# Gate and up of a SwiGLU block as 2 by 2 block products with seven products, on one Trainium2 core

## The reference

```python
h = h + y @ w_out                                   # y: RWKV-7 and attention heads, 2048 wide
hn = rmsnorm(h, ffn_norm_g)
h = h + (silu(hn @ w_gate) * (hn @ w_up)) @ w_down  # 2048 -> 5632 -> 2048
e = rmsnorm(p @ ple_proj, ple_norm_g)               # p: 256 wide
gate = sigmoid(rmsnorm(h, ple_gate_norm_g) @ ple_gate_w + ple_gate_b)
h = h + gate * e
```

## Time and profile before

| | us |
|---|---|
| median of 3 runs | 2743.32 |
| lowest, highest run | 2742.16, 2745.13 |
| span of the profiled execution | 2740.7 |
| busy: PE, PEld, DVE, ACT, POOL | 2685.5, 2142.2, 1167.3, 1022.2, 220.5 |

### The profile page before, as it was taken

The page is one execution under the profiler, slowest core; times in us unless marked ns, Lnnn a source line. Parts: engine busy times, 40 slices in busy tenths (PEclk is TensorE's granted clock), DMA queues, the critical chain, the costliest instruction groups (busy, mean ns, idle before and its releaser), DMA issues.

```text
span 2740.7 us, 41126 instructions
## 1 busy us (share of the span) xinstructions
PE 2685.5 (98%) x15562; PEld 2142.2 (78%) x15562; DVE 1167.3 (43%) x1717; ACT 1022.2 (37%) x1460; POOL 220.5 (8%) x348
## 2 busy tenths in 40 slices
PE   7999999999999999999999999999999999999998
PEld 6776776776776788888888888888888888888787
DVE  6654653653653535333333333333333333334543
ACT  5445535534544425433223332233332222234421
POOL 3101200210111103000000000000000000011300
PEclk9999999999999999999999999999999999999999
DMA  5221231231132323322233222332223322233332
GB/s 169 87 77 63 68 90 59 70 86 63 63 95 95 125 92 108 105 92 99 81 95 108 98 99 82 96 105 99 95 85 95 108 99 92 94 87 108 105 120 75
DMA packets 108136, 255.91 MB, mean 93 GB/s; under 512 B 35288, under 2 KB 37848, under 8 KB 108024
## 3 DMA queue, kind: packets, MB, share of 16 engines
q1 hardware_dynamic: 105920, 247.10, 28.2%
q0 software_dynamic: 2112, 7.34, 0.8%
HBM read 245.43 MB, written 8.98 MB: 93 GB/s over the span
## 4 chain that ended last, share of the span: by engine, by line
PE 71%; issue 18%; POOL 3%; DVE 3%; ACT 2%; DMA 1%; SPq 1%; POOLq 0%; DVEq 0%; ACTq 0%
PE bank L318 23%; PE bank L315 23%; PE bank L319 23%; PE bank L356 1%; POOL probs L1097 1%; POOL scratch_pool L129 1%; DVE w_lo L310 1%; DMA raw<-w_mix 1%; ACT w_hi L303 1%; POOL sg_t L1089 0%; PE bank L481 0%; POOL carried L1124 0%; POOL M_t L1111 0%; PE bank L510 0%; SPq L1319 0%
## 5 line engine op out<-in xcount | busy, mean ns | idle before, releaser
L310 DVE TENSOR_TENSOR w_lo<-raw,w_hi 128x1024 fp32r<-128x1024 f32 (+1 forms) x484 | 546.0, 1130 | 966.2 <-ACT w_hi L303 965.5
L303 ACT ACTIVATE w_hi<-raw 128x1024 fp32r<-128x1024 f32 (+1 forms) x484 | 471.6, 975 | 964.6 <-PE bank L319 941.3
L315 PE MATMUL bank<-hn_hi,w_hi 128*128 128x512 f32 x1664 | 648.1, 389 | 0.0
L319 PE MATMUL bank<-hn_hi,w_lo 128*128 128x512 f32 x1664 | 647.3, 389 | 0.0
L318 PE MATMUL bank<-hn_lo,w_hi 128*128 128x512 f32 x1664 | 647.3, 389 | 0.0
L315 PE MATMUL bank<-in_hi,w_hi 128*128 128x512 f32 x1088 | 455.6, 419 | 30.3 <-DVE in_lo L1689 12.1
L318 PE MATMUL bank<-in_lo,w_hi 128*128 128x512 f32 x1088 | 440.8, 405 | 0.0
L319 PE MATMUL bank<-in_hi,w_lo 128*128 128x512 f32 x1088 | 427.7, 393 | 0.0
L318 PEld LDWEIGHTS bank<-hn_lo,w_hi 128*128 128x128 f32 x1664 | 312.4, 188 | 65.4 <-issue 0.5
L315 PEld LDWEIGHTS bank<-hn_hi,w_hi 128*128 128x128 f32 x1664 | 312.4, 188 | 65.0 <-issue 0.5
L319 PEld LDWEIGHTS bank<-hn_hi,w_lo 128*128 128x128 f32 x1664 | 312.4, 188 | 64.8
(11 more groups left out here) (240 smaller groups left out, 2120.6 us busy)
## 6 DMA issues: line engine op xcount, KB each, us to landing
raw<-w_gu SPq DMA_DIRECT2D x176, 512.0 KB, 3.4
raw<-w_mix SPq DMA_DIRECT2D x116, 512.0 KB, 3.6
raw<-w_down SPq DMA_DIRECT2D x64, 384.0 KB, 3.1
raw<-w_down SPq DMA_DIRECT2D x64, 320.0 KB, 2.8
raw<-ple_gate SPq DMA_DIRECT2D x32, 512.0 KB, 3.5
raw<-w_mix SPq DMA_DIRECT2D x28, 384.0 KB, 3.3
h_t<-xT SPq DMA_DIRECT2D x4, 1024.0 KB, 6.3
out<-h_t POOLq DMA_DIRECT2D x16, 256.0 KB, 2.3
```

What stands on the lines that cost most here:

```text
L303: nc.scalar.activation(w_hi[:, ring_slots(par2, half), 0:cols[half]], raw[:, half, 0:cols[half]], ACT.Copy).then_inc(hi_ready, 1)
L310: nc.vector.tensor_tensor(w_lo[:, s, 0:cols[half]], raw[:, half, 0:cols[half]], w_hi[:, s, 0:cols[half]].bitcast(F32), ALU.subtract).then_ ...
L315: nc.tensor.matmul(out, w_h, x_hi, start=start, stop=False, skip_group_check=True)
L319: return nc.tensor.matmul(out, w_l, x_hi, start=False, stop=stop, skip_group_check=True)
```

## The change

Gate and up, which were two products with the same input, become one product of 2 by 2 blocks. The row blocks of the weights are a gate tile and the up tile of the same 128 features; the column blocks are the even and the odd kt; the input is cut into even and odd kt and into the left and the right 256 tokens. The product of such blocks is formed with seven block products in place of eight (Winograd's form of Strassen's scheme). A block product is 8 kt with three matmuls of 256 columns each, 168 matmuls for a pair of tiles and 7,392 for the 44 pairs.

- The weights: seven blocks of 128 by 1024 per pair are rounded and subtracted. Three are loaded blocks, four are sums that POOL forms (`pool_sums`, 128x1024 each). The four loaded blocks of a pair (`raw_11`, `raw_12`, `raw_21`, `raw_22`) and the four sums lie where `h_t` lay.
- The input: for every two kt ACT writes the scaled values to `hf`, POOL forms four differences of 128x256 (`pool_x_sums`), ACT rounds blocks and differences, and DVE subtracts. `hf` and the differences `t123` have one buffer. The seven inputs lie in `x_a` and `x_c`.
- The results: DVE and ACT combine the banks (`dve_pair`, `act_copy_product`), then come norm factor, SiLU, product and split as before.
- The residual is stored to DRAM (`h_scratch`) and loaded again for the down projection; the activations of all 44 pairs are stored (`act_scratch`) and loaded by chunk, 5.77 MB each. `ple_proj` now stands between gate/up and down, its result is stored and loaded again (`e_scratch`). The down projection is four chunks in a row, and the gate of the embedding follows it directly.

The diff, cut to what the prediction speaks of:

```diff
-CHUNK_SLABS = 2 * CF + OUT_SLABS
-N_PROJ = N_FFN + CHUNKS * CHUNK_SLABS
+PAIRS = D_FF // P
+QUAD = 4
+KP = KT // 2
+TH = SEQ // 2
+PRODUCTS = 7
+RING = 4
+BLOCKS = PRODUCTS * PAIRS
+N_PROJ = N_FFN + BLOCKS // 2
...
+    raw_21 = sb_at(first + 66 * KB, "raw_21", [P, HALF * P])
+    raw_22 = [sb_at(first + (70 + 4 * i) * KB, f"raw_22_{i}", [P, HALF * P]) for i in range(2)]
+    raw_11 = [raw[:, 0, :], sb_at(first + 78 * KB, "raw_11_odd", [P, HALF * P])[:]]
+    raw_12 = raw[:, 1, :]
+    sums = [sb_at(first + (82 + 4 * i) * KB, f"sum_{i}", [P, HALF * P]) for i in range(4)]
...
+    def act_x_scaled(act, o):
+        i = o // 2
+        act.wait_ge(*added_late(o))
+        if i > 0:
+            act.wait_ge(S("x_summed_pool"), KT // 2 + 4 * i)
+            act.wait_ge(S("hn_ready"), 3 * i - 1)
...
+    def act_x_blocks(act, i):
+        act.wait_ge(S("hn_hi_ready"), 2 * i + 2)
+        nc.scalar.activation(x_hi[0][:, i, :], hf[:, 0, 0:TH], ACT.Copy).then_inc(S("in_hi_ready"), 1)
+        nc.scalar.activation(x_c[:, 0:2, i, :], by_half(hf[:, 1, :]), ACT.Copy).then_inc(S("in_hi_ready"), 1)
+
+    def act_x_sums(act, i):
+        act.wait_ge(S("x_summed_pool"), KT // 2 + 4 * i + 4)
+        nc.scalar.activation(x_a[:, 0:3, i, :], t123[:], ACT.Copy).then_inc(S("in_hi_ready"), 1)
...
+    def pool_x_sums(pool, i):
+        b11, b12, b21, b22 = hf[:, 0, 0:TH], hf[:, 0, TH:SEQ], hf[:, 1, 0:TH], hf[:, 1, TH:SEQ]
+        pool.wait_ge(S("hn_hi_ready"), 2 * i + 2)
+        if i > 0:
+            pool.wait_ge(S("hn_ready"), 3 * i)
+        nc.gpsimd.tensor_tensor(t123[:, 0, :], b12, b11, ALU.subtract).then_inc(S("x_summed_pool"), 1)
+        nc.gpsimd.tensor_tensor(t123[:, 2, :], b22, b12, ALU.subtract).then_inc(S("x_summed_pool"), 1)
+        pool.wait_ge(S("x_summed_pool"), KT // 2 + 4 * i + 1)
+        nc.gpsimd.tensor_tensor(t123[:, 1, :], b22, t123[:, 0, :], ALU.subtract).then_inc(S("x_summed_pool"), 1)
+        pool.wait_ge(S("x_summed_pool"), KT // 2 + 4 * i + 3)
+        nc.gpsimd.tensor_tensor(t4[:, i, :], b21, t123[:, 1, :], ALU.subtract).then_inc(S("x_summed_pool"), 1)
...
+    def pe_pair(pe, p, q, first=False):
+        banks = gu_banks(q)
+        for j in range(PRODUCTS):
+            pe.wait_ge(lo_ready, blocks(PRODUCTS * p + j + 1))
+            if j == 0 and not (isinstance(p, int) and p < 2):
+                pe.wait_ge(copied, 3 * p - 3)
+                pe.wait_ge(combined, 7 * p - 7)
+            if j == 3:
+                pe.wait_ge(copied, 3 * p + 1)
+            if j == 5:
+                pe.wait_ge(copied, 3 * p + 2)
+            if j == 6:
+                pe.wait_ge(combined, 7 * p + 3)
+            if first and j == 6:
+                pe.wait_ge(S("hn_ready"), 3 * KP + 1)
+            if first and j == 2:
+                pe.wait_ge(S("h_summed"), KT + 1)
+                nc.tensor.matmul(aux[:], ones[:], acc_h[:], start=True, stop=True, skip_group_check=True
+                                 ).then_inc(S("norm_summed"), 1)
+            out, slot = banks[bank_of[j]][:, 0:TH], gu_slot(q, j)
+            high, low = x_hi[x_of[j]], x_lo[x_of[j]]
+            for i in range(KP):
+                if first and j < 3:
+                    pe.wait_ge(S("hn_ready"), 3 * i + j + 1)
+                w_h, w_l = w_hi[:, slot, i * P:(i + 1) * P], w_lo[:, slot, i * P:(i + 1) * P]
+                nc.tensor.matmul(out, w_h, high[:, i, :], start=opens[j] and i == 0, stop=False, skip_group_check=True)
+                nc.tensor.matmul(out, w_h, low[:, i, :], start=False, stop=False, skip_group_check=True)
+                last = nc.tensor.matmul(out, w_l, high[:, i, :], start=False, stop=i == KP - 1, skip_group_check=True)
+            last.then_inc(weights_used, 1)
...
+    def act_pair(act, p, q, first=False, last=False):
+        for j in range(PRODUCTS):
+            if j in (0, 2, 3):
+                act_copy_product(act, p, q, j)
+            if first and j == 2:
+                rstd_of(act, rstd_h, NORM_FFN)
+            if j == 6:
+                act.wait_ge(combined, 7 * p + 5)
+                if not (isinstance(p, int) and p == 0):
+                    act.wait_ge(S("act_product_ready"), p)
+                nc.scalar.activation(silu_u[:], cg[:], ACT.Silu).then_inc(S("silu_ready"), 1)
+            if not (last and j + RING >= PRODUCTS):
+                act_round_block(act, *ahead(p, q, j))
+            if j == 0 and not (isinstance(p, int) and p == 0):
+                act_high_out(act, p - 1)
...
+    def dve_pair(dve, p, q, first=False, last=False):
+        a, b, c, d = (bank[:, 0:TH] for bank in gu_banks(q))
+        left, right = slice(0, TH), slice(TH, SEQ)
+        had_one = not (isinstance(p, int) and p == 0)
+        for j in range(PRODUCTS):
+            if j == 0 and had_one:
+                dve_product(dve, p - 1)
+            if j == 1:
+                dve.wait_ge(weights_used, blocks(PRODUCTS * p + 2))
+                dve.wait_ge(copied, 3 * p + 1)
+                if had_one:
+                    dve.wait_ge(S("silu_ready"), p)
+                nc.vector.tensor_tensor(cg[:, left], p1_s[:], b, ALU.add).then_inc(combined, 1)
+                if had_one:
+                    dve_low_out(dve, p - 1)
+            if j == 3:
+                dve.wait_ge(copied, 3 * p + 3)
+                nc.vector.tensor_tensor(u5_s[:], u2_s[:], p5_s[:], ALU.add).then_inc(combined, 1)
+            if j == 4:
+                dve.wait_ge(weights_used, blocks(PRODUCTS * p + 5))
+                dve.wait_ge(combined, 7 * p + 2)
+                nc.vector.tensor_tensor(cu[:, right], u5_s[:], d, ALU.add).then_inc(combined, 1)
+            if j == 5:
+                dve.wait_ge(weights_used, blocks(PRODUCTS * p + 6))
+                nc.vector.tensor_tensor(cg[:, right], u2_s[:], c, ALU.add).then_inc(combined, 1)
+                if first:
+                    dve.wait_ge(S("norm_ready"), NORM_FFN)
+                dve.wait_ge(combined, 7 * p + 4)
+                nc.vector.tensor_tensor(cg[:], cg[:], rstd_h[:], ALU.mult).then_inc(combined, 1)
+            if j == 6:
+                dve.wait_ge(weights_used, blocks(PRODUCTS * p + 7))
+                nc.vector.tensor_tensor(cu[:, left], u2_s[:], d, ALU.add).then_inc(combined, 1)
+                dve.wait_ge(combined, 7 * p + 6)
+                nc.vector.tensor_tensor(cu[:], cu[:], rstd_h[:], ALU.mult).then_inc(combined, 1)
+            if not (last and j + RING >= PRODUCTS):
+                dve_subtract_block(dve, *ahead(p, q, j))
...
+    def pool_sums(pool, p, q, which=(1, 2, 3, 4)):
+        s1, s2, s3, s4 = (t[:] for t in sums)
+        a11, a12, a21, a22 = raw_11[q % 2], raw_12, raw_21[:], raw_22[q % 2][:]
+        had_one = not (isinstance(p, int) and p == 0)
+        s_count = lambda k: 4 * p + k
+        if 1 in which:
+            pool.wait_ge(*landing("21", p, q))
+            pool.wait_ge(*landing("22", p, q))
+            if had_one:
+                pool.wait_ge(lo_ready, blocks(PRODUCTS * p - 4))
+            nc.gpsimd.tensor_tensor(s1, a21, a22, ALU.add).then_inc(sum_ready, 1)
+        if 2 not in which:
+            return
+        pool.wait_ge(*landing("11", p, q))
+        pool.wait_ge(sum_ready, s_count(1))
+        if had_one:
+            pool.wait_ge(lo_ready, blocks(PRODUCTS * p - 3))
+        nc.gpsimd.tensor_tensor(s2, s1, a11, ALU.subtract).then_inc(sum_ready, 1)
+        if had_one:
+            pool.wait_ge(lo_ready, blocks(PRODUCTS * p - 2))
+        nc.gpsimd.tensor_tensor(s3, a11, a21, ALU.subtract).then_inc(sum_ready, 1)
+        pool.wait_ge(*landing("12", p, q))
+        pool.wait_ge(sum_ready, s_count(2))
+        if had_one:
+            pool.wait_ge(lo_ready, blocks(PRODUCTS * p - 1))
+        nc.gpsimd.tensor_tensor(s4, a12, s2, ALU.subtract).then_inc(sum_ready, 1)
...
+            act_high_out(act, PAIRS - 1)
 
             act.wait_ge(S("p_landed"), 16)
+            act.wait_ge(lo_ready, blocks(PRODUCTS * (PAIRS - 1) + 5))
+            act.wait_ge(sum_ready, 4 * PAIRS)
             for k in range(2):
-                nc.scalar.activation(p_hi[:, k, :], p_raw[:, k, :], ACT.Copy).then_inc(S("p_hi_ready"), 1)
-            with act.Fori(0, CHUNKS - 1) as c:
-                pairs(act, CF, lambda i, last: gate_up_pair(c, i, last))
-                pairs(act, OUT_SLABS // 2, lambda i, last: down_pair(c, i, last, False))
-            pairs(act, CF, lambda i, last: gate_up_pair(CHUNKS - 1, i, last))
-            pairs(act, OUT_SLABS // 2, lambda i, last: down_pair(CHUNKS - 1, i, last, True))
+                nc.scalar.activation(p_hi[:, k, :], p_raw[:, k, :], ACT.Copy).then_inc(S("act_hi_ready"), 1)
+            act.wait_ge(weights_used, blocks(PRODUCTS * PAIRS))
+            for u in range(PROJ_SLABS):
+                round_slab(act, N_PROJ + u, u, unloaded=UNLOADED)
...
+                if i == KP - 2:
+                    pool.wait_ge(S("x_landed_4"), 16 + 16)
+                    pool.wait_ge(S("hn_hi_ready"), KT - 6)
```

(15 more changed lines are left out.)

623 lines of the change are left out of this document (406 added, 217 removed).

## The result

The changed kernel takes 2752.74 us (median of 5 runs, 2746.78 to 2752.94), the kernel before beside it 2743.23 (2740.96 to 2745.13): a ratio of 1.0031, 95% interval 1.0018 to 1.0044. It is slower by 9.5 us where 39 us of gain were forecast. The time lies inside the range, near the second rival's 2750.

The account below looks back on a forecast made before the run. TensorE's stream of matmuls was taken as the bound. Matmuls -69.9, slips +3, start +18, end +8 and DMAs +2 gave -39 us, from the median 2743.3 to 2704 us; range 2645 to 2770.

Parts of the forecast that it names:

- the second rival: Gate and up: VectorE and POOL become the bound, port time 21.3 us per pair; 2750 us, chance 0.27.
- Matmuls: Gate and up: 7,392 matmuls of 256 columns at 120.2 ns, 888.5 us against 958.4, so -69.9 us.
- Rivals 1: Gate and up: the fixed part belongs to the 512 columns, 113.5 ns per matmul; 2655 us, chance 0.15.
- 3 (a load in series): Gate and up: each matmul waits 188 ns for its weight load; 3202 us, chance 0.08.
- Other engines in a pair: Gate and up: ACT, VectorE and POOL fit beside PE's 20.2 us per pair; +3 us for slips.
- the ratio of 1.62 to 1.98: VectorE and POOL sums side by side: 1.62 us per pair of operations, not 1.98; scaled 21.3 to 17.4 us.
- the 2.32 for a subtraction of 1.23: VectorE subtraction beside POOL sums, 2.32 us instead of 1.23; cited for the second rival.
- its own sign: PE's waits naming `w_lo` or a VectorE-freed bank in every pair, and subtraction mean above 1.6 us, would confirm the second rival.
- The start: Input preparation ahead of gate and up: a chain of 6.8 us per two kt; +18 us, between 8 and 30.
- the 2 us taken: At the start: about 2 us more if the clock falls to 1.2 GHz over the waits.
- The end: End of gate and up: 6.5 us until the projection's first slab is cut, +8 us (5 to 12); projection keeps 24.4.
- DMAs: Down's first chunk: activations and residual loaded through POOL's queue; +2 us (0 to 12).

Follow-up runs that it names:

- run 2: Changed kernel with the weight sums of pairs 1 to 43 left out, GpSimd writing constants by memset instead; 2717.2 us (0.9905).
- run 1: Changed kernel with the four weight sums of pairs 1 to 43 moved from GpSimd to VectorE; 2721.4 us (0.9917).
- run 4: Changed kernel with only the last of four weight sums moved to VectorE in pairs 1 to 43; 2725.9 us (0.9936).
- run 3: As run 2, but GpSimd copies 768 columns of a resident input, one SBUF input, in place of the memset; 2720.4 us (0.9916).
- Run 12: Against run 11, each even residual addition in the late slabs stands ahead of VectorE's input subtractions; 2699.9 us (0.9844).
- run 10: Changed kernel with all weight sums, input differences and sum of squares on VectorE, activations' load later, bank evacuations ahead of the second slab's subtraction; 2705.8 us (0.9867).
- run 11: Against run 10, the first ple_proj slab and the projection's input are rounded and subtracted in the last pair's stages 3 to 5; 2699.1 us (0.9841).

## Why the prediction was wrong, point by point

**Matmuls: right.** -69.9 forecast, -71.4 measured; 120.2 ns taken, 120 found. Rivals 1 (113 ns) and 3 (a load in series) are out.

**Other engines in a pair: the step that failed.** The prediction had the right sum, 11.7 + 9.6 = 21.3 us, and scaled it to 17.4 by the ratio of 1.62 to 1.98, as if the two engines overlapped in part. That ratio was misread. 1.62 is the length of merged rows divided by four, and such a row ends with its last operation, without the wait that would follow. Taken singly, the operations there start 1.70 us apart (kernel before):

```profile
27.59 1.56 POOL L1903 TENSOR_TENSOR acc_x<-acc_x,sqx 128x512 f32<-128x512 f32 x1
...
28.11 1.59 DVE L1703 TENSOR_TENSOR acc_x<-acc_x,sqx 128x512 f32<-128x512 f32 x1
...
29.30 1.56 POOL L1903 TENSOR_TENSOR acc_x<-acc_x,sqx 128x512 f32<-128x512 f32 x1
```

VectorE's ends 0.55 us behind GpSimd's, as behind every sum and copy above, and GpSimd's next one 1.15 us behind VectorE's (1.29 alone). So both waited in full there too, and the 2.32 for a subtraction of 1.23, to which I gave second place, said the same. With 1.70 in place of 1.62 the scaled sum would be 18.3 us and still fit in 20.2: it is the scaling of a shared sum that fails, more than its factor.

Nor was 21.3 the pace. A pair of 20.76 us is VectorE's own queue, 13.1 us of work (run 2), with what is left of the sum at four meetings, 8.5 us; as the rows are drawn with ends that overlap by some 0.07 us, these lengths add up to more than the 20.7 it is busy. What had to be added up is one engine's queue with each meeting's remainder, and compared with the 20.16 of TensorE. Forecast +3, measured +25.0 in the pairs behind the first; runs 1 and 4 take all of that back. A small slip beside it: four operations of a pair read a bank, not three, 0.4 us.

"SBUF — State Buffer" of the Trainium skill (Who interferes with whom) states this exclusion, the later one waiting till the first has ended. The trace agrees with it (2.68 us = 2.12 left of the sum and 0.56), and with its condition of a GpSimd read (runs 2 and 3). I should not have discounted it.

**The rival that came closest.** The second, 2750 us against 2752.7, with the sign and the mechanism right; by its own sign (a bank freed by VectorE in every pair, a subtraction's mean above 1.6 us) it holds, with 1.78. That it came so near is luck, by errors that cancel: it charged 44 x 21.3, 24 us more than 44 x 20.76, and 28 us at both ends where 55 came.

**The start: the place right, the size half.** +18 forecast, 15.6 + 22.6 = 38.2 measured. The chain was 8.25 us per two kt instead of 6.8, by the same exclusion (differences of 0.93, 1.18 and 1.78 us where 0.73 were taken). I let the late slabs run on freely beside it, but VectorE's residual additions stand behind its input subtractions in order, and they came 8.25 us per two instead of 5.44. (Run 12 puts half of them ahead and gains 0.6 us of the stretch, so the order alone isn't what holds them.) TensorE's waits from 1040 to 1165 us were for the weights' low parts, for the additions that free the late slabs' banks and for the input (total, times, longest):

```profile
PE bank L1355 <- DVE w_lo L1323: 9.9, 4, 6.3
PE bank L346 <- DVE h_t L2117: 8.0, 5, 2.5
PE bank L1355 <- DVE x_c L1267: 4.5, 1, 4.5
```

The clock cost more than the 2 us taken. Over the 42.8 us of the first pair it was granted at 0.80 on average; it fell three times, each time while TensorE stood in a wait (4.8, 2.7 and 6.6 us from start to start). Behind these waits the matmuls start 0.21 us apart, which is the lower level, 1.2 GHz:

```profile
1118.03 0.41 PE L1355 MATMUL bank<-x_c,w_hi 128*128 128x256 f32 x1
1118.24 0.41 PE L1356 MATMUL bank<-x_c,w_hi 128*128 128x256 f32 x1
```

Some 60 such distances in the first pair are 5.8 us of its 22.6; the rest are waits. With all of GpSimd's operations there moved (run 10) gate and up begin 6.6 us earlier (6.1 counted from the first residual addition), and the first pair takes 12.7 less; 9.0 and 9.9 us against the kernel before are left, which no run took away.

**The end: +8 forecast, +17.2 measured.** The gap is 5.97 us where 6.5 were worked out, and run 11 removes it. Missed was that the projection, now right behind it, shares the DMA engines with 5.77 MB of activations and takes 35.6 instead of 24.4 us. Its one long wait is 8.4 us, and 15 of its matmuls start 0.43 us apart instead of 0.23 (granted clock 0.81), some 3 us more.

**DMAs: +2 forecast, nothing in the place named.** Down waits for no activations (TensorE is busy for all of its 479.5 us); the price came out in the projection.

## What to carry to other kernels

An engine that is shown as busy may be waiting: compare the same operation's mean with and without the other engine beside it. Where VectorE reads two inputs from SBUF while GpSimd reads SBUF, put GpSimd's remaining time into VectorE's queue in full. Read such a meeting from single rows: a merged row divided by its count hid it here. Work moved onto the fuller engine can make it less full. A pace is a maximum, so a margin of 3% is no margin: 26 us hung on one operation per pair. A change that saves time in a long steady stage is paid at the stage's two ends, and these are chains to be followed row by row, their DMAs and the clock after each wait included.

## What the runs showed of the hardware beyond that

- GpSimd's writes do not hold VectorE (0.95 us memsets beside operations that stayed at 0.68 us); its reads do, with one input as with two. An operation of 512 columns that was held ends 0.55 us behind GpSimd's, whatever was left: 0.32, 1.47, 2.12 or 2.23 us in runs 3 and 4 and the changed kernel, and 1.0 at the start of the kernel before.
- VectorE operations with a bank as one input are untouched: L1431 took 0.42 us with 1.93 us of a sum left (run 4).
- The hold works both ways: GpSimd's fourth sum took 3.32 us where the first took 2.40 for the same columns; one of them began at 1516.33, in a subtraction that lasted till 1517.38.
- A weight load shown as 193 ns passes beside a matmul of 256 columns at 120 ns: of 7,391 distances 7,021 are that.
- Open: why gate and up still begin 9 us later in run 10, where the chain runs at 7.0 us per two kt against 5.44 before and VectorE is busy for 17.7 of the 19.0 us from 1093 on; and whether the projection reaches 24.4 us again with `w_down` ahead of the activations. Neither was tried further.
